# GpSimd's subtraction for the low half of the weights, cut into four instructions of 256 columns

## The reference: what is computed

```python
for l in range(DEPTH):                                   # DEPTH = 2
    mod = c_act @ w_ada[l] + b_ada[l]                    # six vectors of 1024: shift, scale, gate, twice
    h = _modulate(_rmsnorm(x, norm_mix_g[l]), shift1, scale1)
    x = x + gate1 * _mixer(h, w_in[l], w_ret_out[l], w_sb_out[l], w_mix_out[l])
    h2 = _modulate(_rmsnorm(x, norm_mlp_g[l]), shift2, scale2)
    u = jnp.square(jax.nn.relu(h2 @ w_up[l]))            # 1024 -> 4096
    x = x + gate2 * (u @ w_down[l])                      # 4096 -> 1024
return _rmsnorm(x, final_g)
```

## Time and profile before

| | |
|---|---|
| median of 3 runs | 2580.16 us (2579.53 to 2580.59) |
| span of the profiled execution, first to last instruction | 2577.3 us |
| PE busy | 2436.3 us, 95% |
| DVE busy | 1147.3 us, 45% |
| POOL busy | 901.7 us, 35%, of which 899.5 in 368 subtractions |
| ACT busy | 890.2 us, 35% |

### The profile page before, as it was taken

One profiled execution on the slowest core, in us unless ns is written; L12 is line 12 of the kernel. 1 busy time (PEld: TensorE's weight loads), 2 busy tenths in 40 slices (PEclk: granted clock), 3 DMA queues, 4 the chain that ended last, 5 costly groups with the idle time before them and its releaser, 6 DMA issues.

```text
span 2577.3 us, 32158 instructions
## 1 busy us (share of the span) xinstructions
PE 2436.3 (95%) x11946; PEld 1991.6 (77%) x11946; DVE 1147.3 (45%) x1535; ACT 890.2 (35%) x1005; POOL 901.7 (35%) x382
## 2 busy tenths in 40 slices
PE   6999999999998889999979999999999988999898
PEld 5887887888877667777867888888888866777786
DVE  6343243144446872552454323233444487552623
ACT  2222222255582232222322222224556613222232
POOL 1333433433332323433433343333332323433342
PEclk7999999999999999999999999999999998999999
DMA  6222222211125633433222232222112354433421
GB/s 216 92 86 82 96 77 82 95 63 59 62 67 174 200 99 102 144 128 98 98 79 79 73 103 66 90 94 67 64 65 66 98 178 145 145 121 113 130 93 55
DMA packets 252462, 260.62 MB, mean 101 GB/s; under 512 B 4145, under 2 KB 250049, under 8 KB 252353
## 3 DMA queue, kind: packets, MB, share of 16 engines
q1 hardware_dynamic: 250816, 255.92, 30.7%
q10 hardware_dynamic: 1536, 3.17, 0.4%
HBM read 256.97 MB, written 2.10 MB: 101 GB/s over the span
## 4 chain that ended last, share of the span: by engine, by line
PE 73%; DVE 15%; issue 4%; ACT 4%; DMA 3%; DVEq 0%; SPq 0%; ACTq 0%
PE proj L695 45%; PE proj L732 11%; DVE ada_sum L962 8%; PE proj L717 5%; PE att L830 3%; PE att L784 3%; DVE work L1222 3%; PE att L815 2%; PE att L842 1%; PE att L771 1%; DMA w_raw<-in_w_mix_out 1%; DMA work<-in_w_ada 1%; DVE ada_sum L960 1%; ACT w_hi L403 1%; ACT y_hi L606 1%
## 5 line engine op out<-in xcount | busy, mean ns | idle before, releaser
L365 POOL TENSOR_TENSOR w_lo<-w_raw,w_hi 128x1024 fp32r<-128x1024 f32 x368 | 899.5, 2448 | 1637.4 <-ACT w_hi L403 1637.1
L695 PE MATMUL proj<-h_hi,w_hi 128*128 128x512 f32 x1472 | 591.7, 402 | 10.5 <-DVE x_T L1035 9.4
L403 ACT ACTIVATE w_hi<-w_raw 128x1024 fp32r<-128x1024 f32 x368 | 385.3, 1054 | 612.0 <-PE proj L695 443.7
L695 PE MATMUL proj<-h_hi,w_lo 128*128 128x512 f32 x1472 | 578.0, 393 | 0.0
L695 PE MATMUL proj<-h_lo,w_hi 128*128 128x512 f32 x1472 | 577.5, 392 | 0.0
L695 PE MATMUL proj<-y_hi,w_hi 128*128 128x512 f32 x832 | 333.1, 400 | 21.2 <-DVE y_lo L1225 21.0
L695 PEld LDWEIGHTS proj<-h_hi,w_hi 128*128 128x128 f32 x1472 | 279.3, 190 | 72.8 <-issue 13.5
L695 PE MATMUL proj<-y_lo,w_hi 128*128 128x512 f32 x832 | 329.7, 396 | 0.0
L695 PE MATMUL proj<-y_hi,w_lo 128*128 128x512 f32 x832 | 329.5, 396 | 0.0
L695 PEld LDWEIGHTS proj<-h_hi,w_lo 128*128 128x128 f32 x1472 | 278.9, 189 | 59.9
L695 PEld LDWEIGHTS proj<-h_lo,w_hi 128*128 128x128 f32 x1472 | 279.4, 190 | 59.2 <-issue 3.8
(11 more groups left out here) (147 smaller groups left out, 2630.3 us busy)
## 6 DMA issues: line engine op xcount, KB each, us to landing
w_raw<-in_w_in SPq DMA_DIRECT2D x88, 1024.0 KB, 5.1
work<-in_w_ada SPq DMA_DIRECT2D x56, 1024.0 KB, 5.3
w_raw<-in_w_up SPq DMA_DIRECT2D x32, 1024.0 KB, 6.1
w_raw<-in_w_down SPq DMA_DIRECT2D x32, 1024.0 KB, 5.0
w_raw<-in_w_ret_out SPq DMA_DIRECT2D x16, 1024.0 KB, 4.9
w_raw<-in_w_sb_out SPq DMA_DIRECT2D x8, 1024.0 KB, 6.3
w_raw<-in_w_mix_out SPq DMA_DIRECT2D x8, 1024.0 KB, 7.8
ya<-in_x SPq DMA_DIRECT2D x1, 2048.0 KB, 8.3
```

The lines of the kernel that those rows point to most:

```text
L365: pool.tensor_tensor(w_lo[:, s, :, :], w_raw[:, s // 2, :, P * (s % 2):P * (s % 2 + 1)], w_hi[:, s, :, :], ALU.subtract).then_inc(lo_ready, 1)
L403: act.activation(w_hi[:, 2 * s + j, :, :], w_raw[:, s, :, P * j:P * (j + 1)], ACT.Copy).then_inc(hi_ready, 1)
L695: last = pe.matmul(proj[:, j, :], w[:, slot, k, :], a[:, k, :], start=k == 0 and n == 0, stop=k == KT - 1 and n == 2)
```

## The change

GpSimd's loop issues four subtractions of two of the eight k-tiles each (2 x 128 columns) where it issued one of eight k-tiles (1024 columns). The same elements are subtracted; the wait for `hi_ready` stands ahead of the first, and `lo_ready` is counted up by the last.

```diff
                 for s in range(4):
 
                     pool.wait_ge(hi_ready, 4 * v + s + 1)
-                    pool.tensor_tensor(w_lo[:, s, :, :], w_raw[:, s // 2, :, P * (s % 2):P * (s % 2 + 1)],
-                                       w_hi[:, s, :, :], ALU.subtract).then_inc(lo_ready, 1)
+                    for part_of in range(4):
+                        ks = slice(2 * part_of, 2 * part_of + 2)
+                        ins = pool.tensor_tensor(w_lo[:, s, ks, :], w_raw[:, s // 2, ks, P * (s % 2):P * (s % 2 + 1)],
+                                                 w_hi[:, s, ks, :], ALU.subtract)
+                    ins.then_inc(lo_ready, 1)
```

## The result

The median fell from 2579.99 us to 2515.89 us (2515.22 to 2518.1 in four runs); the ratio is 0.9751, with a 95% interval of 0.9737 to 0.9765. The forecast was 2538 us with a range of 2522 to 2580: the direction and the mechanism held, and the gain was 64 us where I had 42.

The account below looks back on a forecast made before the run. VectorE's chain, stopped while GpSimd subtracts, was taken to set the pace where TensorE isn't full. Terms 30 + 2 + 8 + 2 = 42 us off 2577.3 gave 2535 of span, 2538 us as median; range 2522 to 2580.

Parts of the forecast that it names:

- the forecast had 0.53 and 0.34: Time a 0.74 us piece holds VectorE: 0.53 us if both start together, 0.34 us in a chain.
- no record above 1.3 us: Sign of being right: no square L1222 above 1.3 us, where one held by a whole subtraction took 2.50.
- didn't wait for `w_lo`: Later `w_lo` was costed at nothing for TensorE; a new wait for it would show the forecast wrong.
- the port isn't kept over a seam: Denies rival "Slower": GpSimd keeps the port from piece to piece, collisions last 0.4 us longer, 2606 us; chance 0.14.
- a piece doesn't hold for its recorded length: Denies rival "No gain": a piece holds VectorE for all of its recorded 0.74 us, 2579 us; chance 0.11.
- not only the squares: Denies rival "Only the squares gain": 19 us in the `up` stretches and 4 elsewhere, 2557 us; chance 0.20.
- the term for the clock: After `y_lo` waits the granted clock is 0.50; shorter waits may spare it in some of six places: 2 us.
- The cut from a sum that was right: Six `up` stretches with `w_ada`: 5.8 us less each, 35 us, taken as 30 since TensorE's waits limit the gain.
- SB_OUT and MIX: 8 taken: Shorter VectorE stops in SB_OUT and MIX: 5.6 us a layer, 4 taken because of DMA waits and late loads, 8 us.
- The norm: 2 us of gain taken: Norm at a layer's start: L1023, held twice, is held by four pieces at 0.34 us instead; 2 us less.
- my own second forecast: Expectation for the follow-up with eight pieces of 128 columns everywhere: nearly all VectorE stops go, about 2504 us.

Follow-up runs that it names:

- cut in the head alone: Four pieces only in pairs 0 to 25 of each layer (norm, retention, attention), whole subtractions from SB_OUT on, against the kernel before: 2581.26 us, ratio 1.0006.
- The run with the extra matmuls: Kernel before, whole subtractions, plus 12 unread matmuls ahead of TensorE's wait for the last `y_lo` tile in six quarters with `w_ada`: 2565.86 us, ratio 0.9942.
- leaving the head whole: Four pieces only from SB_OUT on (pairs 26 to 45 of each layer), whole subtractions before, against the kernel before: 2519.02 us, ratio 0.9759.
- a quarter of the work: One piece of 256 columns for each half, the rest of `w_lo` left at zero, against the kernel before: 2467.3 us, ratio 0.9559.

## What of the prediction held, and the step that failed

**What held.** VectorE stood still while GpSimd subtracted, with two and four pieces it gets in at the next seam, and the gain is in the stretches where VectorE sets the pace (cut in the head alone: ratio 1.0006). A piece takes 0.74 us. Four pieces hold a chain of seven for 5.22 - 3.61 = 1.61 us, 0.53 for the first and 0.36 for each of the others; the forecast had 0.53 and 0.34. The square has no record above 1.3 us. TensorE didn't wait for `w_lo` anywhere in the changed kernel's trace. None of the rivals came about with four pieces: the port isn't kept over a seam, a piece doesn't hold for its recorded length, and the chains gain too, not only the squares.

**The step that failed is the term for the clock: 2 us taken, 13.3 measured.** The row of 0.50 in the earlier trace rows says 3 us lost at one place, and the forecast took 2 us for all six. The windows of the six down halves (each from its first matmul to that of the next stage) give the size. TensorE is busy 279.0 us in them before and 265.7 after, for the same matmuls, with a granted clock of 0.93 to 0.97 before and 1.00 after. Its waits for `y_lo` there fell from 21.0 to 8.3 us. So of the 26.0 us by which these halves shrank, 13.3 are the clock and 12.7 the shorter wait. The run with the extra matmuls got 11.6 of it back without touching VectorE's chain. One of the six before:

```profile
1060.13:1111.15 51.02, 47.26 (x197) 38.72 (x196) 13.01 (x20) 10.23 (x11) 21.49 (x9) 0.93 0.46 144
```

and the same one after:

```profile
1045.34:1091.00 45.66, 44.32 (x198) 36.42 (x197) 10.62 (x17) 9.60 (x10) 24.95 (x35) 1.00 0.51 161
```

With 13.3 in place of 2 the forecast would have been 2527 us, still inside its range. Only with the next term as well does it pass the low end.

**The cut from a sum that was right.** For the six up stretches I had computed 35 us and taken 30. The up halves gave 23.0 us and the waits of the down halves behind them 12.7, 35.7 together. The cut of 5 had no row behind it.

**SB_OUT and MIX: 8 taken, 13.7 measured** with the MLP norm. Here I had computed 5.6 a layer and taken 4. TensorE's waits there have gone from 17 to 12 us a layer (the list of L684 and of the waits for `x_T`). The granted clock went from 0.91 to 0.95 in the window of the earlier trace rows, but only from 0.93 and 0.94 to 0.94 and 0.95 over the whole of the two stages, in the first and second layer. How the rest divides between fewer stops and the clock isn't settled; no run kept them apart there.

**The norm: 2 us of gain taken, 1.2 of loss measured** over both. The stops themselves came nearly as forecast, but what stands behind them was left out. L1031 (L1028 before), never held before, now is, GpSimd and VectorE alternate through both halves, and GpSimd ends them later. VectorE in the first norm of the changed kernel:

```profile
55.18 1.00 DVE L1026 SCALAR_TENSOR_TENSOR work<-x_T,n_scale,work 128x512 f32<-128x512 f32 x1
56.10 1.22 DVE L1031 SCALAR_TENSOR_TENSOR h_lo<-work,n_shift,h_hi 128x512 fp32r<-128x512 f32 x1
...
70.72 0.69 DVE L1057 TENSOR_TENSOR work<-proj,work 128x512 f32<-128x512 f32 x1 [3.92 <-DMA work<-in_rope]
```

Eight pieces hold eight instructions for 0.25 to 0.48 us, 2.9 us in all, where two whole subtractions held two for 1.9 each, 3.8 in all. The norm does end 0.7 us earlier, but GpSimd is 1.6 us later with its second half, the weight load behind it is issued at 63.85 in place of 62.29, and it now runs beside the rope table. The two traces' DMA views of 60 to 75 us, before and changed (KB, us to landing):

```profile
work<-in_rope ACTq DMA_DIRECT2D x1, 512.0 KB, 3.5
```

```profile
work<-in_rope ACTq DMA_DIRECT2D x1, 512.0 KB, 4.9
```

VectorE starts the rotation 0.8 us later than before, and TensorE waits 2.2 us for its bank. That this transfer is slow because of the other is the reading that fits, not one that a run shows; leaving the head whole gave nothing measurable back.

**The sum.** 35.7 + 13.3 + 13.7 - 1.2 = 61.5 us, and 0.6 of loss in the other stages, 60.9 between the two spans; the median of the runs is 3 us better than that, since the profiled execution was the slowest of its four.

**Why eight pieces beat my own second forecast.** I expected 2504 and got 2483. In the table, the six down halves fall to 264.6 and the up halves to 252.3, which is what a quarter of the work gives (264.1, 251.0), so there TensorE has next to nothing left to win. Of the 35.9 us of span between four pieces and eight, these halves gave 14.5, near the 2.2 us for each of six that I had named. SB_OUT, MIX and the MLP norm gave 15.6 and the start and norm 3.9. I had named some 10 us of waits in SB_OUT and MIX and left most of it out of the 2504. Measuring how long these stretches last when there are no stops would have been better than counting the stops that are left.

## What to carry to other kernels

GpSimd and VectorE held each other up for nearly a whole instruction here. Where the engine with slack (GpSimd) runs long instructions beside a chain of short ones on the engine that sets the pace, cut the long ones, down to where the fixed part (0.18 us here) makes the slack engine late itself. The best size was 128 columns, and twice as fine gave back a third of the gain. Look for it in the durations: the same instruction at 0.68 and at 2.50 us. And price a wait of TensorE with the low clock behind it, from the row that shows it: six waits of 2 to 4 us cost 13.3 us more than their own length.

## What the runs showed of the hardware

- With pieces of 1.29 and 0.74 us, a VectorE instruction that was held up went ahead of the next GpSimd instruction: none was held for longer than one piece. With pieces of 0.46 and 0.33 us this isn't so throughout: instructions were held through six pieces (2.75 us in place of 0.54) and through more than a dozen (4.81 in place of 0.69). The Trainium skill ("SBUF — State Buffer", section "Who interferes with whom") gives an exclusive lock for the whole instruction, and the trace agrees but for its length: a subtraction recorded as 2.40 us holds for 2.19, one of 0.74 us for 0.53.
- GpSimd's memsets don't hold up VectorE's instructions with two inputs (522 ns with and without 272 us of them), but they do hold up its one-input cast to `y_hi` (483 to 799 ns in the mean). The same section of the Trainium skill tells the two kinds apart in this way, and the trace agrees.
- Doing useless work on TensorE during six waits (five of 3.8 us, one of 2.1) made the program 13.3 us faster; the granted clock behind the wait shown was 1.00 in place of 0.50. In the changed kernel waits of 1.3 to 1.5 us at the same places left it at 1.00.
